# Four edits in a two-block network on one core: the modulation's turn, the first mixer's tail, the rope tables and the sums of squares

## The reference

```python
def trunk_layer(xl, xc, c, c_ctx, prm, even, ctx_out, ropes):
    # m = nine vectors from silu(cond) @ mod_w + mod_b, one set for c and one for c_ctx
    x = x + 0.5 * gate0 * swiglu(modulate(rms_norm(x, ffn1_norm), m0, m1), w_in, w_out)
    x = x + gate1 * mixer(modulate(rms_norm(x, mix_norm), m3, m4))
    x = x + 0.5 * gate2 * swiglu(modulate(rms_norm(x, ffn2_norm), m6, m7), w_in, w_out)
...
def rope_tables(positions):
    ang = positions.astype(jnp.float32)[:, None] * freqs[None, :]
    return jnp.cos(ang), jnp.sin(ang)
...
def second_block(x, positions, ...):
    for l in range(DEPTH):
        x = x + 0.5 * swiglu_2(rms_norm_2(x, ffn1_norm[l]), ...)
        x = x + hybrid_mixer(rms_norm_2(x, mix_norm[l]), cos, sin, l, ...)
        x = x + 0.5 * swiglu_2(rms_norm_2(x, ffn2_norm[l]), ...)
    return rms_norm_2(x, final_norm)
```

## Time and profile before

| | |
|---|---|
| three runs | 3400.0, 3400.05, 3398.05 us; median 3400.0 |
| the profiled execution | 3398.24 us |
| its span in the trace | 3396.5 us |
| PE matmul busy, share of the span | 3223.1 us, 95% |
| PE weight load busy | 2865.6 us, 84% |
| DVE, ACT, POOL busy | 2026.9 us (60%), 1428.2 us (42%), 181.8 us (5%) |
| mean granted clock of PE | 0.976 |
| read by the largest DMA queue | 474.88 MB, 49.3% of 16 engines' time |

### The profile page before, as it was taken

How to read it: one execution, slowest core, us unless ns; L and a number is a source line. 1 busy time by engine, 2 the same in 40 slices (tenths; PEclk the granted TensorE clock), 3 DMA queues, 4 the chain that set the end, 5 groups by cost and what they waited for, 6 DMA issues and landing times. The chain is left out here.

```text
span 3396.5 us, 51226 instructions
## 1 busy us (share of the span) xinstructions
PE 3223.1 (95%) x20294; PEld 2865.6 (84%) x20294; DVE 2026.9 (60%) x2665; ACT 1428.2 (42%) x2342; POOL 181.8 (5%) x151
## 2 busy tenths in 40 slices
PE   5999999889999999999889999999999999999998
PEld 4878777468787788877579999899999999999998
DVE  4776759747777633335445566556466665654665
ACT  3333334633333322224454444445454544454543
POOL 1000011000000100020000000300000002100000
PEclk8999999989999999999999999999999999999999
DMA  7566632026666333332136656553556665543664
GB/s 226 156 180 180 172 95 78 13 69 177 176 188 183 101 87 108 88 101 87 50 86 170 178 165 181 157 173 100 148 160 187 177 185 153 166 132 109 177 180 130
DMA packets 769421, 478.28 MB, mean 141 GB/s; under 512 B 37973, under 2 KB 746165, under 8 KB 769093
## 3 DMA queue, kind: packets, MB, share of 16 engines
q1 hardware_dynamic: 767200, 474.88, 49.3%
q10 hardware_dynamic: 2020, 0.64, 0.1%
HBM read 474.40 MB, written 1.05 MB: 140 GB/s over the span
## 5 line engine op out<-in xcount | busy, mean ns | idle before, releaser
L537 PE MATMUL psum<-normed,weights_part 128*128 128x256 f32 (+1 forms) x7392 | 1311.0, 338 | 32.0 <-DVE normed L867 11.6
L537 PEld LDWEIGHTS psum<-normed,weights_part 128*128 128x128 f32 x7392 | 1140.7, 192 | 186.9 <-issue 35.7
L523 DVE TENSOR_TENSOR weights_part<-weights,weights_part 128x2048 fp32r<-128x2048 f32 (+1 forms) x413 | 884.9, 2143 | 365.1 <-ACT weights_part L515 364.8
L515 ACT ACTIVATE weights_part<-weights 128x2048 fp32r<-128x2048 f32 (+1 forms) x413 | 739.1, 1792 | 811.1 <-PE psum L537 418.7
L537 PE MATMUL psum<-hidden,weights_part 128*128 128x256 f32 (+1 forms) x4224 | 680.4, 323 | 0.0
L537 PEld LDWEIGHTS psum<-hidden,weights_part 128*128 128x128 f32 x4224 | 614.5, 191 | 61.2
L537 PE MATMUL psum<-unscaled,weights_part 128*128 128x256 f32 x4224 | 515.3, 285 | 8.9 <-DVE unscaled L675 6.8
L537 PEld LDWEIGHTS psum<-unscaled,weights_part 128*128 128x128 f32 x4224 | 511.2, 193 | 11.4 <-DVE unscaled L675 8.6
L1086 DVE SCALAR_TENSOR_TENSOR stage<-weights,cond,stage 128x768 f32<-128x768 f32 x294 | 281.0, 1018 | 0.0
L406 POOL TENSOR_TENSOR square<-square,rinvs 128x256 f32<-128x256 f32 (+1 forms) x39 | 57.2, 1467 | 2773.6 <-ACT rinvs L391 2772.1
L880 DVE TENSOR_TENSOR rinvs<-rinvs,psum 128x256 f32<-128x256 f32 (+1 forms) x88 | 45.8, 520 | 163.2 <-ACT rinvs L774 163.2
(11 more groups left out here) (445 smaller groups left out, 2650.6 us busy)
## 6 DMA issues: line engine op xcount, KB each, us to landing
weights<-in_l_ffn_w_in SPq DMA_DIRECT2D x176, 512.0 KB, 5.1
weights<-in_ffn_w_gu SPq DMA_DIRECT2D x176, 512.0 KB, 5.0
weights<-in_l_mod_w SPq DMA_DIRECT2D x168, 384.0 KB, 3.4
weights<-in_w_in SPq DMA_DIRECT2D x34, 1024.0 KB, 5.2
weights<-in_w_gate SPq DMA_DIRECT2D x64, 512.0 KB, 5.2
weights<-in_l_ffn_w_out SPq DMA_DIRECT2D x64, 384.0 KB, 4.1
weights<-in_ffn_w_down SPq DMA_DIRECT2D x64, 384.0 KB, 3.9
weights<-in_l_ffn_w_out SPq DMA_DIRECT2D x64, 320.0 KB, 3.3
```

The lines of the kernel that those rows point to most:

```text
L515: k.nc.scalar.activation(k.parts[part][0][:, W], k.slots[slot][:, W], ACT.Copy).then_inc(k.high_done, 1)
L523: k.nc.vector.tensor_tensor(k.parts[part][1][:, W], k.slots[slot][:, W], k.parts[part][0][:, W].bitcast(F32), ALU.subtract).then_inc(k.spl ...
L537: mm = k.nc.tensor.matmul(to, left[a], right[b], start=first and n == 0, stop=last and n == len(PASSES) - 1)
```

## The change

Four edits:

1. **The turn.** In a streamed half FFN PE's transposes of a group no longer stand behind the unit in which they were due but in the middle of the next unit: in an input unit between the gate tile and the up tile, in an output unit ahead of the sixth of its eleven chunks. In the last unit PE waits for ACT's last sum of the stream ahead of the last chunk.
2. **The mixer's tail.** ACT's Sqrt of the convolution's variance stays in slot 23, the reciprocal is cut into four pieces of 128 columns in slots 23 to 26, the first out unit is split in two halves, on ACT in slots 25 and 26, on DVE in slots 27 and 28, and the scaling of the convolution comes in slots 29 to 32. The second out unit is not split here, but in the out projection. The gates are taken in slots 33 and 34, two in each.
3. **The squares.** POOL adds six squares instead of seven (five adds); PE sums three buffers instead of two. `sum_parts` can make a part of these groups ahead of the end; how many is said by `begun`.
4. **The rope tables** (`RopeTables`, as `rope_tables` before, in methods): the positions are loaded where they were, the angles and tables are computed behind the fifth input unit of the half FFN. In its first spec ACT and DVE have no loop now.

```diff
-        for n in range(1, KD - 1):
+        for n in range(1, KD - 2):
             pool.wait_ge(squared.sem, first + n + 1)
...
+def sums_bank(k, last, bank=None):
+    return 2 * ((last + 2) % RING) + 1 if bank is None else bank
+
+
+def sum_parts(k, pe, tokens, bank, some):
+
+
     squared, summed = k.tally("x_squared"), k.tally("x_summed")
+    total, buffers = square_buffers(k, tokens)
+    for n in some:
+        if n == 0:
+            pe.wait_ge(summed.sem, summed.base + KD - 3)
+        else:
+            pe.wait_ge(squared.sem, squared.base + KD - 2 + n)
+        part = (total, buffers[(KD - 2) % 2], buffers[(KD - 1) % 2])[n]
+        for b in range(tokens // P):
+            mm = k.nc.tensor.matmul(k.psum[:, bank, b:b + 1], part[:, b * P:(b + 1) * P], k.const("ones")[:, 0:1],
+                                    start=(n, b) == (0, 0), stop=n == 2, skip_group_check=True)
+    return mm
...
-        pe.wait_ge(summed.sem, chunks_summed)
         pe.wait_ge(k.banks_free, RING + last)
-        for n, part in enumerate((total, buffers[(KD - 1) % 2])):
...
+        sum_parts(k, pe, tokens, sums_bank(k, last), range(begun, 3)).then_inc(t["added"].sem, 1)
...
@@ half_ffn
     late = 1 if depth == 4 else 0
+    begun = 0
...
-            between(act)
+            if between is not None:
+                between.load(act)
...
-                each_unit(act, 0, spec.n, unit_in if s % 2 == 0 else unit_out, looped(s))
+                begun = 0
+                if s == 0 and between is not None:
+                    each_unit(act, 0, BETWEEN, unit_in, looped(s))
+                    between.tables(act)
+                    begun = BETWEEN
+                each_unit(act, begun, spec.n, unit_in if s % 2 == 0 else unit_out, looped(s))
...
+                        if stream is not None and (tile, kc) == (1, 0):
+                            stream.turn(pe, at(spec, c) - 1)
...
                     mm.then_inc(k.unit_done, 1)
-                    if stream is not None:
-                        stream.turn(pe, at(spec, c))
...
+                        if stream is not None and kc == KH // 2:
+                            stream.turn(pe, at(spec, c) - 1)
+                        if s == len(specs) - 1 and c == KD - 1 and kc == KH - 1:
+                            if stream is not None:
+                                stream.wait_summed(pe)
+                            if begun:
+                                sum_parts(k, pe, tokens, sums_bank(k, first + total - 1), range(begun))
...
-        invert_rms(k, block, tokens, first + total - 1, spread, following)
+        invert_rms(k, block, tokens, first + total - 1, spread, following, begun)
...
+    def wait_summed(self, pe):
+
+        pe.wait_ge(self.summed.sem, self.summed.base + len(self.groups))
...
-CONV_MEAN, CONV_VARIANCE, CONV_SCALED = 17, 22, 23
-HEAD_AHEAD = {28: 0, 31: 1}
+CONV_MEAN, CONV_VARIANCE, CONV_ROOT, CONV_SCALED = 17, 22, 23, 28
+OUT_HIGH, OUT_LOW = (25, 26), (27, 28)
...
-    k.ahead[out.name] = 2
+    k.ahead[out.name] = 1
...
-                if s in HEAD_AHEAD:
-                    split_high(k, act, 0, out.start + HEAD_AHEAD[s])
+                if s in OUT_HIGH:
+                    half = out_halves[OUT_HIGH.index(s)]
...
+                    last = nc.scalar.activation(out_part[0][:, half], out_slot[:, half], ACT.Copy)
...
-                    for c in ((0,), (1, 2), (3,), (), ())[s - N_HEAD_JOBS]:
+                    for c in ((), (0, 1), (2, 3), (), ())[s - N_HEAD_JOBS]:
...
-                if s == CONV_SCALED:
+                if CONV_ROOT <= s < CONV_ROOT + 4:
+                    piece = conv_inverse[:, (s - CONV_ROOT) * P:(s - CONV_ROOT + 1) * P]
                     dve.wait_ge(t["conv_root"].sem, t["conv_root"].base + 1)
-                    nc.vector.reciprocal(conv_inverse, conv_inverse).then_inc(t["conv_inverse"].sem, 1)
+                    nc.vector.reciprocal(piece, piece).then_inc(t["conv_inverse"].sem, 1)
```

111 lines of the change are left out of this document (60 added, 51 removed).

## The result

| | before | after |
|---|---|---|
| median of 5 runs | 3400.05 us (3398.05 to 3405.81) | 3385.35 us (3380.75 to 3386.86) |
| ratio, 95% interval | | 0.9947 [0.9935, 0.9958] |
| span of the profiled execution | 3396.5 us | 3379.0 us |

The change is faster by 0.5%: the interval of the ratio is 14 to 22 us of 3400, and the two medians shown are 14.7 us apart. The forecast was 3381.4 us, in a range from 3371 to 3391. The two spans differ by 17.5 us, where the sum on record was 16.8.

What follows compares the result with a forecast made beforehand. PE was taken as the bound, busy 95% of the span, with only 173.4 us idle or slow stretches to win. Terms -3.0, -3.9, -9.3 and -0.6 sum to -16.8 us: 3398.2 to 3381.4, range 3371 to 3391.

Steps and rivals of the forecast that it cites:

- A: Streamed half FFNs, turn moved into the next unit: 22.3 us of stage waits removed, 19.3 of new waits; -3.0 us.
- B: ffn2 of layer 1, rope tables behind unit 4: 2.81 us wait and slow unit go, 0.6 wait comes; -3.9 us.
- C: First mixer's tail: 9.3 us of waits for DVE's scaled rows and 3.9 of slow clock go, 3.9 comes; -9.3 us.
- D: Sums of squares at the ends: POOL's last add goes, a third group of PE sums comes; -0.6 us.
- One sign on record: First mixer's tail, if right: four reciprocals of 0.9 us and no PE wait over 1.5 us.
- The bound of -13.2: First mixer's tail, largest gain: 9.3 us of waits and 3.9 of slow clock, without the 3.9 of ACT delays.
- the rival that held it for harmful: Sums of squares: `begun` stays 0, so the edit misses its aim and gives +5 instead of -0.6, 3387 us; chance 0.05.
- (1): Streamed half FFNs: waits partly turn into larger ones, half the full delay, +11 for the turns, 3395 us; chance 0.13.
- (2): Streamed half FFNs: ACT and DVE have more slack, only 4 us of small waits replace 22.3, 3366 us; chance 0.07.
- (3): First mixer's tail: ACT's halves and gates are passed on in full, -5 there, 3385.7 us; chance 0.05.
- (4): Rope tables and mixer's tail: a table switch holds ACT 2.6 us, twice its load, +2.6 in each, 3386.6 us; chance 0.02.
- (5): Streamed half FFNs: DVE never catches up, each of 14 turns passes on 5.5 us, +54.7, 3439 us; chance 0.02.

## Why the prediction was right

Differences in us; the third column is from the one pair of profiles, the fourth from undoing the part and, where said, from the averages over several profiles.

| | on record | before to after | by the experiment |
|---|---|---|---|
| A, turns | -3.0 | +1.6 | -4.2 (-1.6 between averages; -4 with the clock left out) |
| B, tables | -3.9 | -4.0 (with its end's third group) | -4.55 |
| C, tail | -9.3 | -13.5 (-14.9 less D's -1.4) | -11.4 (-9.9 to -13.4) |
| D, squares | -0.6 | -1.6 by the stretches, +0.1 by the ends (another +0.7 lies ahead of the first edit) | -1.6 by the ends on average; +0.9 to +2.3 in the conditioning, -0.5 to -1.7 at each end that waits for POOL |

**A.** The mechanism is the one on record, to a few tenths: waits of 1.24 and 3.10 us at the units named, none at the third turn, and DVE's wait 7.7 us. The term left out is the clock. Behind the 3.10 us wait PE runs at the lower level, and that costs 1.7 us a time. The same is true of the 3.4 us waits that went, so between the two kernels most of it cancels; in one pair of profiles it need not, and here it turned -4.1 into +1.6. That the sum of the four parts still came to 17.5 is luck: C gained more in this pair than it does on average, and A less. By the averages the four are -1.6, some -4 to -5, -11.6 and -1.6, about -19, inside the 14 to 22 us of the ratio's interval and 2 us over the sum on record.

**B.** Right in place, and in size but for the one profile of 212.5 us. Two details were wrong: the 0.6 us wait behind the tables did not come, and the number of table loads did not stay 3, it is 1. Both come from one thing, that Sin runs from the table that is loaded for Silu. The working had ACT reload twice, 2.6 us that were never needed.

**C.** The three waits went, as said, and 0.67 of the first stayed. One sign on record failed: a wait of 1.88 us stands in the tail, where none was to be over 1.5. The term that was mis-sized is the new waits for ACT: they came to 1.2 us, where 3.9 were set. The clock's part, set at 3.9, is 3.8 between the averages. In this one pair it looks larger, 6.4 against nothing: before there are four stretches (from 657, 674, 684 and 694 us), and the last of them follows a 2.60 us wait that the edit keeps. After there are none, but seven of the eight profiles with the new tail have one to three there, behind the waits of 1.88 and 2.60 us that are left. The bound of -13.2 was no bound for a single pair, since the clock's part had been estimated and then taken as fixed.

**D.** About right in sum, by terms of both signs. The prediction named the second block's mixers as two of the four ends where PE waits for POOL; they are the ends of its two ffn1. In the conditioning the third group cost 2.0 to 2.3 us in this pair (from the first sum to the Sqrt 4.25 us, against 1.95 before and 2.22 with two groups again), since PE comes to the lower clock there, where eight of these sums take 1.85 us; at the full clock it costs the 0.9 on record (2.81 against 1.91 us from the last product to the Sqrt). That `begun` does nothing was read rightly from the order, and the rival that held it for harmful was wrong: making it work costs 20 us in the half FFNs.

**The rivals.** (1), larger waits of DVE and PE in the streams: no. (2), no new waits: no, though the version with six late turns shows what it would have been worth: its two half FFNs take 25 us less than before. (3), ACT's halves passed on in full: no, 1.2 us in all. (4), the drain: not seen, 0.03 us beside the 1.28 us load at the switches of the run with the tables back. (5), DVE never catching up: no, the third turn of each half waits for nothing.

## What to carry to other kernels

When a wait is moved from one engine to another, ask at each of its places who was waiting for whom: here the same edit was right at six places, where PE waited for the group, and wrong at four, where DVE waited for PE, and doing only the six brought 27 us more. A wait that is removed is worth its length and, for waits like the 3.1 us ones here, in most executions the slow clock behind it. Work that fills an unavoidable wait must stay behind the product that the wait belongs to, not in front of it.

## What the runs showed of the hardware

The lower clock behind a wait of PE is in part a matter of chance, even at the same place of the same program. In six of the profiles PE has the 3.10 us wait four times each; a stretch at granted clock 0.5 (1.2 GHz) follows 20 of these 24 waits. Of the 3.4 us waits for the stage in the profiles before and with the turns back, it follows 5 of 8. A wait of 2.66 us in the second mixer of the first block is followed by one in 1 of 12 profiles, a wait of 7.2 to 7.9 us in the same mixer has one in 12 of 12. A stretch takes 3.4 us, or a multiple of it, and costs 1.7 for each 3.4 where PE is busy. So one profile against another can be off by some 5 us in the stretch that an edit touched, without the edit (first out projection 257.2 to 260.7 us, ffn2 of layer 1 206.6 to 212.5); it took the sum over many executions, or the same stretch in seven profiles, to size the parts here.

All 60 table loads of ACT in the profile before take 1.283 us, and in the kernels with the tables ahead the instructions on both sides of Sin's and Silu's loads stand within 0.02 us of them. Sin behind Silu needed no load, Silu behind Sin did.
